# Softmax results turned by VectorE and DMAs in place of TensorE, in a hybrid attention layer on one core

## The reference, cut to what matters

```python
h = rms_norm(x, norm_mix)
qa, ka, va, qf, kf, vf, f_logit = split(h @ w_in)
# group A: 4 key/value heads for 16 query heads, rotary, window of 128 keys in chunks of 64, a sink per head
w = softmax over the window's keys and the sink; o = w @ va
# group B: s = q k^T / 8 + F[t] - F[s], F = cumsum(log f), causal
p = softmax(s); o = p @ vf
x = x + concat(out_a, out_b) @ w_o
h = rms_norm(x, norm_ffn)
x = x + (silu(conv(h @ w_up)[gate]) * conv(h @ w_up)[val]) @ w_down
out = rms_norm(x, norm_final)
```

## Time and profile before

| | us |
|---|---|
| median of 3 runs | 1049.02 |
| lowest, highest | 1048.55, 1051.02 |
| the profiled execution | 1050.31 |
| its span (first to last instruction) | 1048.5 |
| DMA traffic | 259.5 MB, 248 GB/s in the mean |
| TensorE's granted clock, mean | 0.998 of full |

### The profile page before, as it was taken

The page is one execution under the profiler, slowest core; times in us unless marked ns, Lnnn a source line. Parts: engine busy times, 40 slices in busy tenths (PEclk is TensorE's granted clock), DMA queues, the critical chain, the costliest instruction groups (busy, mean ns, idle before and its releaser), DMA issues.

```text
span 1048.5 us, 16225 instructions
## 1 busy us (share of the span) xinstructions
PE 1036.2 (99%) x5205; PEld 866.0 (83%) x5205; DVE 803.6 (77%) x1070; ACT 742.5 (71%) x1201; POOL 86.6 (8%) x150
## 2 busy tenths in 40 slices
PE   8999999999999999999999999999999999999997
PEld 8888888888888888888888888888888878878885
DVE  5678676767799678677787787877868999877777
ACT  6956464646456687888878888798887766646663
POOL 1000000011111111111111111111111000000000
PEclk9999999999999999999999999999999999999999
DMA  9675656587789998989898898989888588888992
GB/s 284 193 231 158 192 158 183 154 261 206 219 259 268 281 260 282 247 278 264 251 284 240 277 256 272 262 270 267 257 256 259 172 295 302 295 295 273 317 319 103
DMA packets 146600, 259.52 MB, mean 248 GB/s; under 512 B 10852, under 2 KB 50628, under 8 KB 146432
## 3 DMA queue, kind: packets, MB, share of 16 engines
q1 hardware_dynamic: 128720, 215.32, 62.2%
q0 software_dynamic: 17360, 43.22, 19.1%
q10 hardware_dynamic: 480, 0.47, 0.2%
HBM read 256.86 MB, written 44.06 MB: 287 GB/s over the span
## 4 chain that ended last, share of the span: by engine, by line
PE 91%; DVE 5%; DMA 2%; issue 1%; ACT 1%; SPq 0%; DVEq 0%; ACTq 0%
PE pj L1459 12%; PE pj L1461 12%; PE pj L1460 12%; PE pj L1471 9%; PE tr_ps L1460 8%; PE tr_ps L1461 8%; PE tr_ps L1459 8%; PE pj L1473 5%; PE sc_ps L1459 3%; PE sc_ps L1461 3%; PE sc_ps L1460 3%; PE pj L1486 3%; DVE split L1286 2%; PE pj L1488 1%; DMA raw<-w_down 1%
## 5 line engine op out<-in xcount | busy, mean ns | idle before, releaser
L961 DVE TENSOR_TENSOR split<-raw,split 128x1024 fp32r<-128x1024 f32 x265 | 321.9, 1223 | 159.6 <-ACT split L601 154.4
L601 ACT ACTIVATE split<-raw 128x1024 fp32r<-128x1024 f32 x259 | 272.4, 1055 | 102.4 <-PE pj L1461 32.9
L894 ACT ACTIVATE split<-raw 128x1024 fp32r<-128x1024 f32 (+1 forms) x125 | 121.0, 988 | 67.9 <-PE pj L1461 30.1
L1286 DVE TENSOR_TENSOR split<-raw,split 128x1024 fp32r<-128x1024 f32 (+1 forms) x125 | 138.3, 1136 | 33.8 <-ACT split L894 31.8
L1471 PE MATMUL pj<-act_split,split 128*128 128x512 f32 x416 | 148.1, 400 | 0.0
L1459 PE MATMUL pj<-split,act_split 128*128 128x512 f32 (+1 forms) x384 | 146.2, 381 | 0.7 <-DVE split L970 0.7
L1461 PE MATMUL pj<-split,act_split 128*128 128x512 f32 (+1 forms) x384 | 146.2, 381 | 0.0
L1460 PE MATMUL pj<-split,act_split 128*128 128x512 f32 (+1 forms) x384 | 146.1, 381 | 0.0
L1459 PE MATMUL tr_ps<-split,act_split 128*128 128x512 f32 x352 | 136.9, 389 | 0.0
L1460 PE MATMUL tr_ps<-split,act_split 128*128 128x512 f32 x352 | 136.9, 389 | 0.0
L1461 PE MATMUL tr_ps<-split,act_split 128*128 128x512 f32 x352 | 136.9, 389 | 0.0
(11 more groups left out here) (236 smaller groups left out, 1725.6 us busy)
## 6 DMA issues: line engine op xcount, KB each, us to landing
raw<-w_up SPq DMA_DIRECT2D x176, 512.0 KB, 5.6
raw<-w_in SPq DMA_DIRECT2D x72, 512.0 KB, 3.8
raw<-w_down SPq DMA_DIRECT2D x68, 512.0 KB, 5.8
t_dram<-w_down POOLq DMA_DIRECT2D x60, 512.0 KB, 6.5
raw<-t_dram SPq DMA_DIRECT2D x40, 512.0 KB, 5.9
raw<-w_o SPq DMA_DIRECT2D x32, 512.0 KB, 5.5
t_dram<-t_dram POOLq DMA_DIRECT2D x40, 256.0 KB, 6.0
raw<-w_down SPq DMA_DIRECT2D x20, 256.0 KB, 5.9
```

Source lines behind the costliest of these rows:

```text
L601: ins = act.activation(hi[:, slot, 0:TILE], raw[:, slot, 0:TILE], ACT.Copy)
L894: act.activation(hi[:, slot, c0:TILE], down_raw(t)[:, c0:TILE], ACT.Copy).then_inc(hi_done, 1)
L961: dve.tensor_tensor(lo[:, slot, 0:n], raw[:, slot, 0:n], hi[:, slot, 0:n].bitcast(F32), ALU.subtract).then_inc(lo_done, 1)
L1286: dve.tensor_tensor(lo[:, slot, c0:TILE], down_raw(t)[:, c0:TILE], hi[:, slot, c0:TILE].bitcast(F32), ALU.subtract).then_inc(lo_done, 1)
```

## The change

VectorE turns the softmax results in 32x32 pieces, with keys 4i + b of a row of 128 in piece b; TensorE's transposes and ScalarE's copies are gone. A turned piece still lies on the 32 partitions of its queries' block. Four DMAs for each of three parts take the 32 partitions of block a, in rows of 1 KB (part A) or 768 bytes, to all 128 partitions, so that row 4i + b holds key 4i + b. They write into `prob`, where the softmax results were. The DMAs are issued by SyncE between the weight loads, seven steps after the turning by SyncE's count (its load for tile s + 7 goes out as VectorE works on step s). TensorE's value products, the evacuation and what follows come three tiles later, read the new layout (`turned_a`, `turned_f`) and wait for the DMAs' semaphores. VectorE turns at steps 16, 17 and 18. SyncE's first head group is written out in front of its loop, since it has no DMAs. In the output projection (1, 2) and (1, 4) now come ahead of (0, 3) and (0, 7), so that column group 0 ends at position 11 in place of 9.

```diff
-WO_ORDER = [(0, 0), (0, 1), (0, 2), (0, 4), (0, 5), (0, 6), (1, 0), (1, 1), (0, 3), (0, 7),
-            (1, 2), (1, 4), (1, 5), (1, 6), (1, 3), (1, 7)] + [(n, p) for n in (2, 3) for p in range(PAIRS)]
+WO_ORDER = [(0, 0), (0, 1), (0, 2), (0, 4), (0, 5), (0, 6), (1, 0), (1, 1), (1, 2), (1, 4),
+            (0, 3), (0, 7), (1, 5), (1, 6), (1, 3), (1, 7)] + [(n, p) for n in (2, 3) for p in range(PAIRS)]
-TURN_A = NEXT + 1
-TURN = {NEXT + 2: 0, NEXT + 3: 1}
-PE_VALUES = NEXT + 4
-EVACUATE = NEXT + 5
+TURN_A = NEXT
+TURN = {NEXT + 1: 0, NEXT + 2: 1}
+OUT_A = TURN_A + LEAD + RING
+OUT = {s + LEAD + RING: p for s, p in TURN.items()}
+PE_VALUES = NEXT + 7
+EVACUATE = NEXT + 8
+        turned_a = flat[:, 0:1024].rearrange("p (a h g x) -> p a h g x", a=SIDE, h=2, g=2)
+        turned_f = flat[:, 1024:2560].rearrange("p (r a h t i) -> p r a h t i", r=2, a=SIDE, h=2, t=3)
+        quarters = ((0, 8), (1024, 6), (1792, 6))
...
+            def blocks_out(part, q, landed):
+
+                c0, n = quarters[part]
+                sp.wait_ge(pt_s, q * 3 + (part + 1))
+                for a in range(SIDE):
+                    sp.dma_start(flat[:, c0 + a * n * BLOCK:c0 + (a + 1) * n * BLOCK],
+                                 prob_t[a * BLOCK:(a + 1) * BLOCK, c0:c0 + n * P].rearrange("p (b x) -> p b x", b=SIDE)).then_inc(landed, 16)
...
-                if s == TURN_A:
-                    act.wait_ge(pt_ps, q * 3 + 1)
-                    act.activation(prob_t[:, 0:1024].rearrange("p (h n) -> p h n", h=2), tr_ps[:], ACT.Copy).then_inc(pt_s, 1)
-                if s in TURN:
-                    p = TURN[s]
-                    act.wait_ge(pt_ps, q * 3 + (p + 2))
-                    act.activation(turned_f[:, p], tr_ps[:, :, 0:384], ACT.Copy).then_inc(pt_s, 1)
...
+            def turn_quarters(part):
+
+                c0, n = quarters[part]
+                rows = flat[:, c0:c0 + n * P].rearrange("p (k i b) -> p b k i", k=n, b=SIDE)
+                cols = prob_t[:, c0:c0 + n * P].rearrange("p (b k i) -> p b k i", k=n, b=SIDE)
+                dve.transpose(cols, rows).then_inc(pt_s, 1)
...
             def values_a(q):
 
-                pe.wait_ge(pt_s, q * 3 + 3)
-                for v, c0, c1, moving in ((0, 0, 2, lambda h: turned_a[:, h, :, :, 0:64]),
-                                          (1, 2, 3, lambda h: turned_a[:, h, 1:2, :, 64:128]),
-                                          (2, 3, 4, lambda h: turned_a[:, h, 0:1, :, 64:128])):
+                pe.wait_ge(d_pa, q * PARTS_A + PARTS_A)
+                banks = [tr_ps[h * HD:(h + 1) * HD, 0].rearrange("k (e c a i) -> k a c e i", e=2, c=4, a=2) for h in range(2)]
+                for a in range(2):
                     for h in range(2):
-                        dst = tr_ps[h * HD:(h + 1) * HD, 0].rearrange("k (e c n) -> k c e n", e=2, c=4)[:, c0:c1]
-                        ins = pe.matmul(dst, vq[:, v], moving(h), start=v == 0, stop=True, skip_group_check=True)
+                        pe.matmul(banks[h][:, a, 0:2], vq[:, 0], turned_a[:, a, h].rearrange("p g x -> p (g x)"),
+                                  start=a == 0, stop=True, skip_group_check=True)
+                for v, c, g in ((1, 2, 1), (2, 3, 0)):
+                    for h in range(2):
+                        ins = pe.matmul(banks[h][:, :, c], vq[:, v], turned_a[:, 2:4, h, g],
+                                        start=False, stop=True, skip_group_check=True)
...
+                pe.wait_ge(d_pf, q * PARTS_F + PARTS_F)
...
-                            ins = pe.matmul(tr_ps[h * HD:(h + 1) * HD, 1, p * S + k * P:(p + 1) * S], vf[:, k, i * HD:(i + 1) * HD],
-                                            turned_f[:, p, h, k * S:S + k * P], start=p == 0 and k == 0, stop=k == 1,
-                                            skip_group_check=True)
+                            dst = tr_ps[h * HD:(h + 1) * HD, 1, p * S:(p + 1) * S].rearrange("k (t a i) -> k a t i", t=2, a=SIDE)
+                            ins = pe.matmul(dst[:, :, k:2], vf[:, k, i * HD:(i + 1) * HD], turned_f[:, p, :, h, 2 * k:2 + k],
+                                            start=p == 0 and k == 0, stop=k == 1, skip_group_check=True)
```

More of the change, by code:

```diff
@@ L123 @@
 SQUARES_DONE = SIDE * SIDE
+PARTS_A, PARTS_F = 16 * SIDE, 2 * 16 * SIDE
 WO_TILES = len(WO_ORDER)
@@ L344, in program @@
             "va_s", "never_s", "sa_s", "sf_s", "maxa_s", "expa_s", "read_s", "negmax_s", "exp_s", "proba_s", "prob_s"))
-        pt_ps, pt_s, pv_s, mixhi_s, mixlo_s = (sem(n) for n in ("pt_ps", "pt_s", "pv_s", "mixhi_s", "mixlo_s"))
+        pt_s, d_pa, d_pf, pv_s, mixhi_s, mixlo_s = (sem(n) for n in ("pt_s", "d_pa", "d_pf", "pv_s", "mixhi_s", "mixlo_s"))
         y_s, yturn_s, yhi_s, ylo_s, ysq_s, y2_tot, y2_root, r2_s, r2_out, d_r2 = (sem(n) for n in (
@@ L392, in program @@
         prob_f = flat[:, 1024:2560].rearrange("p (a b n) -> p a b n", a=2, b=2)
-        turned_a = prob_t[:, 0:1024].rearrange("p (h g e n) -> p h g e n", h=2, g=2, e=2)
-        turned_f = prob_t[:, 1024:2560].rearrange("p (a b n) -> p a b n", a=2, b=2)
+        turned_a = flat[:, 0:1024].rearrange("p (a h g x) -> p a h g x", a=SIDE, h=2, g=2)
+        turned_f = flat[:, 1024:2560].rearrange("p (r a h t i) -> p r a h t i", r=2, a=SIDE, h=2, t=3)
+        quarters = ((0, 8), (1024, 6), (1792, 6))
         y_turned = [flat[:, i * 1024:(i + 1) * 1024].rearrange("p (k n) -> p k n", k=4) for i in range(2)]
@@ L432, in load, with attention, load_unit @@
                 sp.dma_start(dst, src).then_inc(d_w[slot], 16)
-            def load_unit(t, w, col):
+            def blocks_out(part, q, landed):
[4 more added lines that the diff above has]
+                                 prob_t[a * BLOCK:(a + 1) * BLOCK, c0:c0 + n * P].rearrange("p (b x) -> p b x", b=SIDE)).then_inc(landed, 16)
+            def attention(s, q):
+                if s == OUT_A:
+                    blocks_out(0, q, d_pa)
+                if s in OUT:
+                    blocks_out(1 + OUT[s], q, d_pf)
+            def load_unit(j, n, col, attend):
                 for kt in range(4):
-                    load(t + kt, kt, narrow(raw, kt), w[kt][:, :, bass.ds(col, 256)])
+                    load(j * QUAD_TILES + (T_QUAD + 4 * n + kt), kt, narrow(raw, kt), win[kt][:, :, bass.ds(col, 256)])
+                    if attend:
+                        attention(4 * n + kt + NEXT, j - 1)
             for kt in range(4):
@@ L453, in _, with quad @@
                 sp.dma_start(dst, src).then_inc(d_tab, 16)
-            with sp.Fori(0, QUADS) as j:
+            def quad(j, attend):
                 for n, col in enumerate((COL_QA, COL_KF, COL_QF, COL_VF)):
-                    load_unit(j * QUAD_TILES + (T_QUAD + 4 * n), win, j * 256 + col)
+                    load_unit(j, n, j * 256 + col, attend)
                     if n == 2:
@@ L462, in _ @@
                                      nft_dram[bass.ds(j * 4, 4)].partition_broadcast(P)).then_inc(d_bias, 16)
+            quad(0, False)
+            with sp.Fori(1, QUADS) as j:
+                quad(j, True)
             for s, (n, pair) in enumerate(WO_ORDER):
                 load(T_WO + s, s % RING, wide(raw, s % RING), wo[pair][:, :, n * 512:(n + 1) * 512])
+                attention(s + NEXT, QUADS - 1)
             with sp.Fori(0, UP_PAIRS) as j:
@@ L1087, in attention @@
                                       ALU.mult).then_inc(proba_s, 1)
+                if s == TURN_A:
+                    dve.wait_ge(proba_s, q + 1)
+                    turn_quarters(0)
                 if s in DVE_NORM:
@@ L1097, in attention @@
                     ins.then_inc(prob_s, 1)
+                if s in TURN:
+                    p = TURN[s]
+                    dve.wait_ge(prob_s, q * 2 + (p + 1))
+                    turn_quarters(1 + p)
                 if s == JOIN_VALUES:
@@ L1532, in scores_ready @@
                     pe.wait_ge(expa_s, j)
-                    pe.wait_ge(pt_s, j * 3)
                     pe.wait_ge(mixlo_s, j * 2)
```

## The result

The changed kernel takes 1059.37 us (median of 4 runs, 1058.38 to 1061.72), the kernel before 1049.36 beside it: ratio 1.0093, 95% interval 1.0073 to 1.0113. It is slower, where 1041.0 was forecast in a range of 1039.5 to 1045.5. The profiled execution took 1059.48 us, its span 1057.7, 9.2 more than before.

A forecast was written before the change was run, and what follows sets the result against it. TensorE was taken as the bound, waiting for nothing in the attention stage. Terms of -8.7, +0.2 and +0.45 us summed to -8.05, giving 1041.0 us against the median of 1049.0, range 1039.5 to 1045.5.

The forecast's parts named there:

- part 2: VectorE takes over three transposes a head group, 3.15 to 4 us, and has room for them: no cost.
- The sum of the three has 5.4 us: Room for VectorE's three transposes in a group before its split for tile 22 makes TensorE wait.
- XA + 2XF: VectorE's time a group for one transpose of 128x1024 and two of 128x768, taken as 3.15 to 4 us.
- Rivals 1 and 3: VectorE late after the softmax: 1045 to 1047 us, chance 0.13; moved pieces landing late: 1052 us, chance 0.06.
- The signs of being wrong: TensorE waiting over 1.5 us in total for splits between 80 and 310 us, or at all for the pieces.
- Part 1: TensorE in the attention stage: transposes removed save 8.7 us; extra value matmuls cost 0.2 us.
- rival 4: Value matmuls slow down by their shorter runs of words, 2.3 us more a group: 1050 us, chance 0.03.
- Part 3: ScalarE loses two kinds of copies and its waits for TensorE; it was not late, so 0.
- Part 4: Twelve DMAs a group on SyncE's queue, 0.37 us an issue, 8.4 us for a landing: no cost.
- Rival 3: The slower side: pieces land late and TensorE waits at the values; 1052 us at 11.2 us landing, chance 0.06.
- Part 5: Later evacuation costs 0; the new order of output tiles costs 0.45 us (0 to 1.5).
- the jam in the output projection: VectorE's work for column groups 0 and 1 falls together; its split for tile 20 is 0.30 us late.

The follow-up runs named there:

- the run with contiguous reads: Changed kernel with VectorE's transposes reading words one after the other, leaving keys in the wrong order; 1047.55 us, ratio 0.9989.
- the joining first: Changed kernel with VectorE's joining of the values at step 16 ahead of the first transpose, not step 18 behind the third; 1041.71 us, ratio 0.992.
- the late joining: Kernel before with six unused 128x1024 reductions on VectorE at steps 16 to 18, the last two ahead of the joining; 1065.4 us, ratio 1.0155.

## Why the prediction was wrong

**The step that failed** is in part 2: "Is there room?", "The sum of the three has 5.4 us" and "Tiles 20 and 21 have more. Nothing". I measured the room of VectorE by its splits alone. In the very sum the joining stands, with its 0.8 us, as something that delays a split; who waits for the joining itself was not asked. By the prediction's own terms it ends at 142.13 + 1.14 + 1.23 + 1.14 + 0.8 + (XA + 2XF) = 146.4 + (XA + 2XF), and TensorE wants it at tile 20, 141.98 + 2 x 2.78 = 147.5. The room was 1.1 us and not 5.4. Even at the 3.15 us that I took the joining would be 2.0 late; the run with contiguous reads has 1.7. At the 5.14 us that were measured it would be 4.0 late; the changed kernel waited 3.6 to 3.7 in each of three groups, 10.9 in all. In the kernel before it had ended at 147.07, for a tile at 149.69: with 2.6 us of cover nothing of it stood in the waits. The row was in the earlier trace rows, the wait in the code.

**A size was off beside it.** XA + 2XF was taken as 3.15 to 4 and is 2.04 + 2 x 1.55 = 5.14 us, 2.0 ns a column. The sentence on the Trainium skill's section 5.2 (Vector Engine (DVE) Microarchitecture Reference) had it: its 1.73 to 2.5 ns a column, which the page gives for two-source operations, hold for the 2.0 ns of this transpose too, and 5.14 us lie within the estimate of 4.4 to 6.4. The run with contiguous reads has 1.21 to 1.26 ns, so the step makes the difference. I had named it and gone by the nearest row. This alone would have cost nothing: 5.14 is under 5.4, and with the joining first TensorE waits for no split at tile 22.

**A term was missing,** the clock after idle time: 6.4 of 18.4 us between forecast and result. Rivals 1 and 3 priced a wait at its length only. The signs of being wrong did not have this case either: they name waits for splits and for the pieces, and in the stage TensorE waited for neither.

**The rest, point by point.** Part 1: the transposes' 8.7 us and the near nothing for the values hold. With the joining first the kernel is 7.9 us faster, 1041.7 against the 1041.0 forecast, and the values of A, now 16 records, take from 274.30 to 275.23, 0.93 us where the twelve of the earlier trace rows took 0.92. The extra matmuls and the shorter runs of words cost nothing that shows (rival 4 falls):

```profile
274.30 0.66 PE L1603 MATMUL tr_ps<-prob 128*64 128x128 f32 x8
274.79 0.61 PE L1607 MATMUL tr_ps<-prob 128*64 128x128 f32 x8
275.23 1.47 PE L1620 MATMUL tr_ps<-prob,vf 128*64 128x256 f32 x16
```

Part 3 holds. Part 4: TensorE never waited for the pieces in the changed kernel, nor for a split that a late load had held. ScalarE did wait more for w_o, in all 20.0 us against 5.1, inside its slack; an issue takes 0.63 us in a batch and not 0.37 (four in 2.5 us), and a landing 2.7 to 2.8 us of the 8.4 that had been reckoned. Rival 3 falls. Part 5: the jam in the output projection came as worked out, 0.23 us at tile 20 for the 0.30. VectorE's time line of the changed kernel has the same order at the same distances as the sum that was continued from the earlier trace rows:

```profile
299.84 1.28 DVE L1187 TENSOR_TENSOR nat<-pj,nat 128x512 f32<-128x512 f32 x2
301.15 3.16 DVE L1198 STREAM_TRANSPOSE prob<-nat 32x256 f32<-32x256 f32 x7
304.32 1.22 DVE L981 TENSOR_TENSOR split<-raw,split 128x1024 fp32r<-128x1024 f32 x1
305.58 1.33 DVE L1198 STREAM_TRANSPOSE prob<-nat 32x256 f32<-32x256 f32 x3
306.93 1.68 DVE L1207 SCALAR_TENSOR_TENSOR act_split<-prob,cst,act_split 128x256 fp32r<-128x256 f32 x4
308.52 1.22 DVE L981 TENSOR_TENSOR split<-raw,split 128x1024 fp32r<-128x1024 f32 x1
```

The evacuation "for four operations: 0" was right in the changed kernel, where TensorE waits for no mix_lo, and 1.0 us short once the wait at tile 20 was gone: the copies stand behind a split that waits for a load. The forecast of the time was thus the right number for a kernel with one step in another place, and the slower side had been given to the DMAs, which had no part in the loss.

## What to carry to other kernels

When work is put onto an engine, list every semaphore that it raises behind that work and find each one's waiter and its time, not only the one that the engine raises most often; a wait with cover does not appear in a list of waits. Releases that free a bank for the bottleneck belong ahead of new work; moving this one cost nothing that shows. A wait of the matmul engine has to be priced with the pace behind it, which the windows show as granted clock.

## What the runs showed of the hardware

- Idle time costs more than its length. Waits of 3.6 to 3.7 us were followed by 5 to 9 pairs of matmuls at a granted clock of 0.50, 0.64 us a pair for 0.35; waits of 2.2 to 2.3 us by a shorter stretch; waits of 1.6 to 1.7 us in the same place by none. The length is not all: in the kernel before with the late joining, waits of 3.37 and 3.43 us were followed by some five slow pairs each and one of 3.30 us by none. Filling the waits with matmuls kept the clock at 1.00 and gave back 6.4 us.
- VectorE's 32x32 transpose of 128x1024 float32 takes 1238 ns with the source in sequence and 2040 with a step of four words, 0.78 ns a word more. If an earlier instruction could write the order that the transpose reads, that would be worth 2.0 us of VectorE a group; this was not tried with a right order of keys.
- DMAs between partitions of SBUF, 96 to 128 KB from 32 partitions to 128, landed in 2.7 to 2.8 us beside weight loads, and 48 of them made no difference to the time that could be measured.
